# The mixers of two layers: taps, norms and the last group sum in another order

## The reference

```python
a_val, a_gate, q, _, _, u, sv, bg, cg, xin = z          # z = modulate(rms_norm(x)) @ w_in, ten parts of 256
y_a = silu(layer_norm(depthwise_conv(a_val * sigmoid(a_gate), conv_a_w) + b))     # 31 taps
y_b = rms_norm(attention(q1, k1, v) - lam * attention(q2, k2, v), subln_g) * (1 - lam_init)   # 4 heads of 64
y_c = gelu(u) * (sg_w @ layer_norm(gelu(sv)) + sg_b)    # chunks of 128 tokens
y_d = bg * depthwise_conv(cg * xin, conv_d_w)           # 3 taps
return concatenate([y_a, y_b, y_c, y_d]) @ w_out
```

## Time and profile before

| What | us |
| --- | --- |
| median of 3 runs (2414.63, 2419.2, 2420.31) | 2419.2 |
| the profiled execution's own time | 2420.38 |
| its span | 2418.5 |
| TensorE busy | 2325.7 |
| VectorE busy | 1686.9 |
| ScalarE busy | 1012.6 |

### The profile page before, as it was taken

How to read it: one execution, slowest core, us unless ns; L and a number is a source line. 1 busy time by engine, 2 the same in 40 slices (tenths; PEclk the granted TensorE clock), 3 DMA queues, 4 the chain that set the end, 5 groups by cost and what they waited for, 6 DMA issues and landing times.

```text
span 2418.5 us, 31469 instructions
## 1 busy us (share of the span) xinstructions
PE 2325.7 (96%) x12378; PEld 1950.9 (81%) x12378; DVE 1686.9 (70%) x2755; ACT 1012.6 (42%) x1585; POOL 31.7 (1%) x65
## 2 busy tenths in 40 slices
PE   7999999999999999999899999999999999988998
PEld 4888877877787888887778999667788888768998
DVE  7776566456578887778778778687675455686655
ACT  3422232247634322323555545565431332466543
POOL 0000000010000000000000000000000000000000
PEclk9999999999999999999999999999999999999999
DMA  8355534453352444443414564212245454223554
GB/s 350 108 194 208 192 139 179 171 189 123 117 196 88 157 176 164 148 148 109 139 45 139 184 197 164 70 53 72 85 165 203 146 183 169 93 83 108 190 184 131
DMA packets 99419, 360.33 MB, mean 149 GB/s; under 512 B 11128, under 2 KB 14584, under 8 KB 97352
## 3 DMA queue, kind: packets, MB, share of 16 engines
q1 hardware_dynamic: 94888, 341.46, 40.5%
q0 software_dynamic: 4384, 16.86, 2.0%
HBM read 350.94 MB, written 5.24 MB: 147 GB/s over the span
## 4 chain that ended last, share of the span: by engine, by line
PE 78%; DVE 13%; ACT 5%; issue 2%; DMA 1%; SPq 1%; DVEq 0%; ACTq 0%
PE PS L616 60%; DVE w_lo L1897 4%; PE PS L644 3%; PE PS L817 3%; PE PS L1033 2%; ACT w_hi L1249 2%; PE PS L859 1%; PE PS L1224 1%; PE PS L833 1%; DVE conv L2704 1%; DMA raw<-in_weights 1%; ACT probs L1759 1%; PE PS L676 1%; DVE xv L2329 1%; DVE h_lo L2319 1%
## 5 line engine op out<-in xcount | busy, mean ns | idle before, releaser
L1897 DVE TENSOR_TENSOR w_lo<-raw,w_hi 128x1024 fp32r<-128x1024 f32 (+1 forms) x456 | 543.3, 1210 | 290.4 <-ACT w_hi L1249 288.8
L1249 ACT ACTIVATE w_hi<-raw 128x1024 fp32r<-128x1024 f32 (+1 forms) x456 | 460.6, 1041 | 486.1 <-PE PS L616 447.8
L616 PE MATMUL PS<-h_hi,w_hi 128*128 128x256 f32 (+1 forms) x1472 | 480.8, 334 | 4.6 <-DVE h_lo L2319 3.1
L616 PE MATMUL PS<-h_hi,w_lo 128*128 128x512 f32 (+1 forms) x1416 | 475.4, 336 | 0.0
L616 PE MATMUL PS<-h_lo,w_hi 128*128 128x512 f32 (+1 forms) x1352 | 457.0, 338 | 0.0
L616 PEld LDWEIGHTS PS<-h_hi,w_hi 128*128 128x128 f32 x1472 | 273.4, 188 | 34.4 <-issue 2.7
L616 PE MATMUL PS<-hid_hi,w_hi 128*128 128x512 f32 (+1 forms) x864 | 289.7, 335 | 2.6 <-DVE w_lo L1897 1.7
L616 PEld LDWEIGHTS PS<-h_hi,w_lo 128*128 128x128 f32 x1416 | 266.9, 188 | 28.0
L616 PE MATMUL PS<-hid_hi,w_lo 128*128 128x512 f32 (+1 forms) x864 | 288.7, 334 | 0.0
L616 PE MATMUL PS<-hid_lo,w_hi 128*128 128x512 f32 (+1 forms) x864 | 288.4, 334 | 0.0
L616 PEld LDWEIGHTS PS<-h_lo,w_hi 128*128 128x128 f32 x1352 | 255.1, 189 | 28.3 <-issue 0.2
(11 more groups left out here) (434 smaller groups left out, 3759.5 us busy)
## 6 DMA issues: line engine op xcount, KB each, us to landing
raw<-in_weights SPq DMA_DIRECT2D x434, 512.0 KB, 4.5
ada_ring<-in_ada SPq DMA_DIRECT2D x176, 512.0 KB, 3.7
raw<-in_weights SPq DMA_DIRECT2D x22, 384.0 KB, 4.1
qk<-in_ada SPq DMA_DIRECT2D x4, 1024.0 KB, 11.3
xv<-in_ada SPq DMA_DIRECT2D x8, 512.0 KB, 12.6
m_hi<-h_spill POOLq DMA_DIRECT2D x4, 1024.0 KB, 8.1
wgt<-in_x SPq DMA_DIRECT2D x2, 1024.0 KB, 19.6
h_spill<-h_hi POOLq DMA_DIRECT2D x1, 2048.0 KB, 7.5
```

The source lines that it names most:

```text
L616: mm = pe.matmul(out, a, b, start=(k == 0 and i == 0), stop=(k == ph.k_tiles - 1 and i == 2))
L1249: act.activation(w_hi[:, s, 0:w], raw[:, s, 0:w], ACT.Copy).then_inc(sem("w_hi"), 1)
L1897: dve.tensor_tensor(w_lo[:, s, 0:w], raw[:, s, 0:w], w_hi[:, s, 0:w].bitcast(F32), ALU.subtract)\
```

## The change

The diff, whole. In words:

- Layer 1, taps: behind the weight splits of `kv1` VectorE makes 24 taps where it made 6, so 40 stand there instead of 22. The two taps at the end of the steps 6 to 12 go; the one that is left is made at the end of step 11.
- Layer 1, conv norm: the sum of the two conv tiles moves from step 14 to step 12, mean and subtractions (VectorE) from 14 to 12, squares (ScalarE) from 14 to 13, the sum of squares from behind step 15 to step 14, the root from behind step 15 to step 14, and the multiplications (`conv_normed`) to VectorE's step 14. `gate_mixed` gets a wait for the first subtraction. The 10 fillers in step 14 go.
- Layer 1, first head pair: ScalarE squares it in step 14 instead of 13, behind the root of the conv norm; the group sum goes to bank 4 instead of 5.
- Both layers: `z_tile(15)` is made right behind `z_tile(14)`, ahead of the wait for `sg_used`.
- Both layers: the group sum of the second head pair, with its wait for `ot`, moves from before the output projection to between its two k-halves, and the 12 fillers ahead of it go. ScalarE's order behind step 15 stays, but for the conv norm's Ln and Exp, which in layer 1 have moved.

```diff
--- before.py
+++ after.py
@@ -116,7 +116,6 @@
 Z_STEPS = (tuple(range(16)), (0, 1) + tuple(range(6, 16)))
 ROPE_AT = ((4, 0), (4, 1), (5, 0), (5, 1), (7, 0))
 ATT_BANK, ATT_TMP, ATT_COL = (0, 1, 6), (0, 1, 6), (8, 16, 0)
-GROUP_SUM_AT = (11, 14)
 LN_EXP = "natural_log_exp_and_others"
 
 
@@ -239,7 +238,7 @@
 assert dotted_before("dkv") + ADA0 <= 3 * ADA_LAYER
 assert dotted_before("kv0") + ADA0 >= 3 * ADA_LAYER and dotted_before("zg1") == len(ADA_MACS)
 
-nsq_after = list(np.cumsum([8, 8, 2, 3, 16, 8] + [8, 2, 1, 2, 1, 8] * 2 + [8]).tolist())
+nsq_after = list(np.cumsum([8, 8, 2, 3, 16, 8] + [8, 2, 1, 2, 1, 8] + [8, 2, 2, 1, 1, 8] + [8]).tolist())
 
 
 
@@ -1160,8 +1159,10 @@
                 for i in Z_STEPS[l]:
                     if l == 0 and i == 0:
                         first_pair()
-                    elif l or i > 1:
+                    elif i < 15 and (l or i > 1):
                         z_tile(i)
+                    if i == 14:
+                        z_tile(15)
                     if i == 0:
                         keys_and_values()
                     if i == 1:
@@ -1184,12 +1185,18 @@
                         group_sum(4)
                     if i == 12:
                         gate_turned()
+                        if l:
+                            sum_two(lambda j: conv[:, j, r], "conv_in")
                     if i == 13:
+                        if l:
+                            pe.wait_ge(sem("n2_xc"), 4 * l + 3)
                         gate_mixed()
                     if i == 14:
                         pe.wait_ge(sem("sg_used"), 2 * (l + 1))
-                        keep_busy(10 * l, 4)
-                        sum_two(lambda j: conv[:, j, r], "conv_in")
+                        if l:
+                            sum_squares(2, 5, r, ones[:], n)
+                        else:
+                            sum_two(lambda j: conv[:, j, r], "conv_in")
                     if i in SCORE_AT[l]:
                         scores(SCORE_AT[l].index(i))
                     if i in TURN_AT[l]:
@@ -1198,12 +1205,10 @@
                         if at and at % per_head == 0:
                             values(at // per_head - 1)
                     if i == 14 and l == 1:
-                        group_sum(5)
+                        group_sum(4)
                 values(3)
-                sum_squares(2, 5, r, ones[:], n)
-                pe.wait_ge(sem("ot"), 2 * l + 2)
-                keep_busy(12, 6)
-                group_sum(6)
+                if l == 0:
+                    sum_squares(2, 5, r, ones[:], n)
                 item[0] += len(slots)
                 y_hi, y_lo = (lambda p: y_part[0](Y_ORDER[p])), (lambda p: y_part[1](Y_ORDER[p]))
 
@@ -1231,6 +1236,9 @@
                     for g in range(2):
                         for m in range(2):
                             y_products(g, m, c)
+                    if c == 0:
+                        pe.wait_ge(sem("ot"), 2 * l + 2)
+                        group_sum(6)
                 residual_product(f"wo{l}", y_hi, y_lo, full, False)
                 feed_forward(f"g{l}", full, 5 + 2 * l)
 
@@ -1838,15 +1846,17 @@
                             square(z[:, 12 + j, r], n)
                     if i == 10:
                         root(RSTD[:, r], 5, r, CTX)
-                    if i == GROUP_SUM_AT[l] - 1:
-                        act.wait_ge(sem("ot"), 2 * l + 1)
-                        square(z[:, 0, r], n)
-                    if i == GROUP_SUM_AT[l]:
-                        root(z[:, 2, r], 4 + l, r, 64)
-                    if i == 14:
+                    if i == 13 + (not l):
                         for j in range(2):
                             act.wait_ge(sem("n2_xc"), 4 * l + 2 + j + 1)
                             square(conv[:, j, r], n)
+                    if i == 14 and l:
+                        root(RSTD[:, r], 5, r, CTX)
+                    if i == (10, 14)[l]:
+                        act.wait_ge(sem("ot"), 2 * l + 1)
+                        square(z[:, 0, r], n)
+                    if i == (11, 14)[l]:
+                        root(z[:, 2, r], 4, r, 64)
 
                 y_hi(0)
                 y_hi(1)
@@ -1856,12 +1866,14 @@
                 act.preload_act_table_set(LN_EXP)
                 y_hi(2)
                 split_to(wo.u0 + 3)
-                root_ln(RSTD[:, r], 5, CTX)
+                if l == 0:
+                    root_ln(RSTD[:, r], 5, CTX)
                 act.wait_ge(sem("ot"), 2 * l + 2)
                 square(z[:, 1, r], n)
                 y_hi(3)
                 root_ln(z[:, 3, r], 6, 64)
-                root_exp(RSTD[:, r], nsd[0] - 1)
+                if l == 0:
+                    root_exp(RSTD[:, r], nsd[0] - 1)
                 root_exp(z[:, 3, r], nsd[0])
                 y_hi(4)
                 split_to(wo.u0 + 4)
@@ -2761,6 +2773,12 @@
                     dve.wait_ge(sem("att_o"), att0 + 2 * j + 2)
                     dve.tensor_copy(z[:, j, r], PS[:, 6, r]).then_inc(sem("ot"), 1)
 
+                def conv_normed():
+
+                    rstd()
+                    for j in range(2):
+                        dve.tensor_tensor(conv[:, j, r], conv[:, j, r], RSTD[:, r], ALU.mult).then_inc(sem("conv_n"), 1)
+
                 def y_slot(p):
 
                     if 8 * l + p - 3 > 0:
@@ -2803,7 +2821,7 @@
                     split_to(LIN["kv1"].u0 + 4)
                     convolve(12)
                     only_split("kv1")
-                    convolve(6)
+                    convolve(24)
                 for at, i in enumerate(Z_STEPS[l]):
                     scored = l and i in SCORE_AT[l]
                     if i % 2 == 0 and not scored:
@@ -2862,14 +2880,16 @@
                                               PS[:, 4 + j, r].rearrange("p (c q) -> p c q", q=P), bias, ALU.add)\
                                 .then_inc(sem("sg_used"), 1)
                     if l:
-                        convolve((2 if i < 13 else len(taps)) if i >= 6 else 0)
+                        convolve(len(taps) if i == 11 else 0)
                     elif i >= 4:
                         convolve((1 if i in SCORE_AT[l] else 6) if i < 13 else len(taps))
-                    if i == 14:
+                    if i == 14 - 2 * l:
                         mean(CTX, r)
                         for j in range(2):
                             dve.tensor_tensor(conv[:, j, r], conv[:, j, r], MEAN[:, r], ALU.subtract).then_inc(sem("n2_xc"), 1)
+                    if i == 14:
                         if l:
+                            conv_normed()
                             rstd()
                             y_diff(0)
                         short_conv(0)
@@ -2886,9 +2906,8 @@
                 split_to(wo.u0 + 3)
                 y_lo(4)
                 split_to(wo.u0 + 4)
-                rstd()
-                for j in range(2):
-                    dve.tensor_tensor(conv[:, j, r], conv[:, j, r], RSTD[:, r], ALU.mult).then_inc(sem("conv_n"), 1)
+                if l == 0:
+                    conv_normed()
                 rstd()
                 y_lo(5)
                 y_diff(1)
```

## The result

The changed kernel takes 2439.16 us (median of 4 runs, 2432.83 to 2442.03) against 2419.76 us before: a ratio of 1.0082, 95% interval 1.0065 to 1.0098, 19.4 us slower. The forecast was 2435 us.

What follows compares the result with a forecast made beforehand. TensorE, busy 96% of the span, was taken as the bound. Layer 0's 5.2, layer 1's 6.0 and the clock's 5.0 made 16.2 us over the median 2419.2 us: 2435 us, range 2423 to 2443.

Steps and rivals of the forecast that it cites:

- steps 1 to 3: Layer 0: tile 15 early, low part 3 at 1660.0, ScalarE's Ln of the last group sum 8.65 us later; +5.2 us.
- the waits: Both layers, without clock dips: 5.2 us in layer 0 and 6.0 us in layer 1, 11.2 us.
- steps 4 to 7: Layer 1: taps hidden, conv sum +0.55 us, new wait of 3.6 us at `gate_mixed`, `y_diff(0)` 1.5 us late.
- step 8: Layer 1, first half of the output projection and the group sum behind it: chain 6.0 us later, layer 1 +6.0 us.
- The signs: Trace checks, among them TensorE idle over 2 us before the first half and 6 to 8 us after the second group sum.
- The clock: TensorE's new gaps in both layers: three dips to the low clock at 1.7 us each, 5 us; bounds 0 and 8.5 us.
- The clock stays at 2.4 GHz: Rival: TensorE keeps full clock in all new gaps; 11.2 us, 2430 us; chance 0.2.
- more is lost: Rival: all dips land on work (8.5 us), and taps outlast cover or steps 6 to 11 yield nothing; 2441 to 2443 us; chance 0.1.
- The first half is not held by the short convolutions: Rival: the output projection's first half starts when TensorE is free; 2420 us, no change; chance 0.13.
- The rival on the faster side: First half starts when TensorE is free and only y tile 4 is exposed after the group sum; 2412 us; chance 0.07.
- the table load: ScalarE's Silu load in the exposed chain: no drain by the rows; the skill's drain would cost layer 0 1.4 us more.
- the prediction's pattern: TensorE's clock: 2.45 us idle alone kept 2.4 GHz; 2.27 and 1.11 us close together, and 3.57 us, did not.

Runs made afterwards that it cites:

- fillers: The changed kernel with filler matmuls put into TensorE's new gaps in both layers, all waits kept: 2431.02 us.
- late_ln: The changed kernel with ScalarE's Ln and Exp of the last group sum behind y tile 6's high part, VectorE's low parts 5, 6 ahead of `y_diff(1)`: 2429.28 us.
- gs_only: The kernel before with only the last group sum moved between the k-halves in both layers, its 12 fillers dropped: 2435.18 us.
- gs_back: The changed kernel with the last group sum, its wait for `ot` and its 12 fillers back ahead of the first k-half, both layers: 2430.96 us.
- combo: The kernel before with tile 15 ahead, early taps, layer 1's 10 fillers removed, 14 fillers ahead of the wait for `ot` replacing 12 behind: 2406.77 us.
- z15_only: The kernel before with only tile 15 made right behind tile 14 in both layers: 2420.98 us.

## Why the prediction was right, point by point

- **Layer 0, steps 1 to 3.** On the old clock I had low part 3 at 1660.0, the group sum's end at 1670.0, the last low part at 1679.5; the trace has 1659.9, 1670.0 and 1679.4. My +5.2 us for the waits stands against +5.4 with fillers and +6.6 with the dips. `late_ln` shows the mechanism: ScalarE's order.
- **Layer 1, steps 4 to 7.** Cover of the taps 1.4, measured 1.65. The last tap at 2162.6: 2166.05 + 0.48, less the 3.95 us that this trace is late at the memset, is 2162.6. The wait for the mean 3.6 us, measured 3.18 in the changed kernel. `y_diff(0)` 1.5 us late, measured 1.4 with fillers.
- **Layer 1, step 8.** +6.0 us, measured +7.4 with fillers, one dip of which was left.
- **The signs.** The idle time after the second group sum, which I put at 6 to 8 us in pieces, was 5.8 us in layer 0 and 4.6 in layer 1. The idle time of over 2 us before the first half came true in layer 0 only (3.80); in layer 1 it was 0.96, since TensorE had made `values(3)` at the low clock.
- **The clock** is the term that was mis-sized. I took three dips of 1.7 us, 5 us, and 8.5 as the bound. The stages give 1.4 us in layer 0 (6.6 less 5.2) and 8.0 in layer 1 (14.0 less 6.0), 9.4 in all; against `fillers` they give 7.8, and the medians 8.1. So it stood at my bound. Where it came in, in layer 1, less the 3.95 us: the gate's product starts 3.0 us later than I had it (2176.3 against 2173.3), `y_diff(0)` 5.8 us later, low part 3 still 5.8, and the group sum ends 7.8 us later. So the two dips of steps 12 to 14 cost about 3 us each where I had 1.7 for a dip (the scores, transposes and values product of step 12 take 6.55 us against 3.73 for the same work from 2151.43 on), and the third another 2.0 in the first half.
- **Why these dips were longer** is open. The two of steps 12 to 14 lasted 6 to 7 us each and took about 3.4 us of full-speed work each, where the dip of the earlier trace rows takes 1.7. Behind the two gaps of the earlier trace rows stood fillers, or the conv sum and projection matmuls; here the scores, transposes and the values product, or the gate's products, scores and transposes, stood first. That this difference is the cause was not tried. Nor was another possible cause, that a dip's length varies with nothing changed around it: `gs_only` has the same work around its wait at the gate as the kernel before, and there the 20 filler records took 4.09 us instead of 3.48; and in `gs_back`, with the work of the changed kernel, the second of these dips lasted from about 2174 to 2184. The row of `gs_only`:

```profile
2192.01 4.09 PE L676 MATMUL PS<-ones 128*128 128x128 f32 x20 [3.58 <-DVE z L2861]
```

- **The rivals.** "The clock stays at 2.4 GHz" fell (0.50 in the rows); its price, 2430 us, is what `fillers` measured, 2431.0. The clock cost that "more is lost" named, 8.5 us, came true, without its other term: the taps stayed under their cover. "The first half is not held by the short convolutions" fell: TensorE waited 3.80 us for low part 0 in layer 0 and 0.96 in layer 1. The rival on the faster side fell with ScalarE's order; `combo` shows that gains in these places were there, but from the parts that the new waits covered.
- Of the sum 16.2, the waits were 11.2 and measured at most 12.8 (`fillers`, one dip still in it); the clock was 5 and measured 8 to 9. The total came out 3.2 us below the measured 19.4. The rest of the span, 1.7 us longer, says nothing: in the other ten profiles it differs from the kernel before by -1.6 to +1.3.
- On the table load the exposed chain of layer 1 decides again (ScalarE's timeline after):

```profile
2217.02 1.28 ACT L1884 ACT_TABLE_LOAD   x1
2218.32 0.60 ACT L1884 ACTIVATE xv<-conv,vec 128x256 f32<-128x256 f32 x1
```

Silu starts 0.02 us after the load's 1.28. The drain of 1.38 us that the Trainium skill (ScalarE: Activation LUTs, What ACT_TABLE_LOAD costs) adds isn't seen here either.

What stays open: how much of layer 1's loss is the conv sum's place in step 12 and how much the wait for its mean in step 13; the two were not taken apart. `combo` and `gs_back` differ by 17 us in that layer, in these two, their dips, the order of the first head pair, and the fillers.

## What to carry to other kernels

When a small reduction is moved to a later point on the engine that bounds the kernel, read what the engine that consumes it has queued behind the consuming instruction: here Ln stood ahead of the high parts of the four y tiles that the next products needed, and the move cost 17 us by itself, and, in the changed kernel, a few moved lines on ScalarE and VectorE took 9.9 us back. Fillers go ahead of the wait that they are to bridge, not behind it. And a new wait on TensorE costs its length plus what the slow clock takes from the work behind, here about 3 us at each of two waits.

## What the runs showed of the hardware that I had not expected

After the gaps of 1.93 and 0.91 us in layer 1 the granted clock stayed at 0.50 (1.2 GHz) from about 2168 to 2174 us with TensorE busy for 2.00 of each 2.00 us, about twice as long as after the gaps of layer 0 before the change, where the stretch after 1647 was near full speed again (0.97). And it fell in `gs_back` during the 5.5 us of idleness, so that the first work behind it, fillers included, was slow from its first instruction.

The length of the idle spell alone does not say whether the clock falls, which is more than the prediction's pattern had: 3.57 us lost it before the change, 1.94 us lost it in `z15_only` (with 1.55 us ahead of `values(3)` shortly before), and in `combo`, with fillers up to the spell, 3.76 us left it at 1.00. The stretches are from the kernel before, then `gs_back`, then `combo`:

```profile
1647.00:1649.00 2.00, 2.00 (x10) 1.58 (x10) 1.93 (x4) 1.21 (x2) 0.00 (x0) 0.97 0.81 236
1650.00:1652.00 2.00, 0.00 (x0) 0.00 (x0) 1.97 (x4) 1.98 (x3) 0.00 (x0) 0.86 0.00 0
1658.00:1660.00 2.00, 2.00 (x8) 1.31 (x9) 1.71 (x2) 1.24 (x3) 0.00 (x0) 1.00 0.00 0
```
